# First block: last three output tiles in token halves, norm and new x by halves beneath them, gate-up started by halves, squares added by VectorE

## What is computed

```
mixed = concat(rms_norm(out_a, group_norm_a), rms_norm(out_b, group_norm_b)) @ w_out
x = x + rms_norm(mixed, norm_mix_post)
h = rms_norm(x, norm_ffn_pre)
f = (silu(h @ w_gate) * (h @ w_up)) @ w_down        # 1024 -> 2816 -> 1024
x = x + rms_norm(f, norm_ffn_post)
```

## Time and profile before

| what | value |
|---|---|
| median of 3 runs | 1234.2 us |
| the profiled execution | 1236.36 us |
| its span, first to last instruction | 1234.6 us |
| TensorE matmul busy | 1140.7 us (92%) |
| VectorE busy | 669.2 us (54%) |
| ScalarE busy | 499.5 us (40%) |
| GpSimd busy | 155.5 us (13%) |
| mean granted TensorE clock | 0.973 of full |

### The profile page before, as it was taken

The page is one execution under the profiler, slowest core; times in us unless marked ns, Lnnn a source line. Parts: engine busy times, 40 slices in busy tenths (PEclk is TensorE's granted clock), DMA queues, the critical chain, the costliest instruction groups (busy, mean ns, idle before and its releaser), DMA issues.

```text
span 1234.6 us, 14658 instructions
## 1 busy us (share of the span) xinstructions
PE 1140.7 (92%) x5104; PEld 918.3 (74%) x5104; DVE 669.2 (54%) x1054; ACT 499.5 (40%) x823; POOL 155.5 (13%) x162
## 2 busy tenths in 40 slices
PE   6897968949999999999978998699999999999996
PEld 5675857737888888888856887577888888888884
DVE  6776885677444444433348787736444444443332
ACT  5785776334333232322234366734332323232221
POOL 1475763021000000000003002200000000000001
PEclk9999989969999999999989999989999999999998
DMA  7311100412322222322221221003222222222311
GB/s 255 115 52 44 52 27 1 162 43 76 111 85 102 88 99 102 102 102 102 102 94 36 93 94 69 1 2 136 85 102 102 97 90 101 86 102 103 102 51 68
DMA packets 31465, 106.04 MB, mean 86 GB/s; under 512 B 4032, under 2 KB 4672, under 8 KB 31296
## 3 DMA queue, kind: packets, MB, share of 16 engines
q1 hardware_dynamic: 31088, 104.99, 24.6%
q10 hardware_dynamic: 336, 0.52, 0.2%
HBM read 100.78 MB, written 2.10 MB: 83 GB/s over the span
## 4 chain that ended last, share of the span: by engine, by line
PE 77%; DVE 11%; ACT 6%; issue 4%; DMA 0%; ACTq 0%; DVEq 0%; POOL 0%; SPq 0%
PE bank L456 23%; PE bank L457 23%; PE bank L458 23%; DVE hl L1469 2%; PE bank L897 1%; PE bank L887 1%; DVE ta L1461 1%; ACT wh L370 1%; DVE xres L1463 1%; DVE wl L378 1%; DVE q L1063 1%; DVE pr L952 1%; ACT pr L1398 1%; ACT pr L1100 1%; ACT pth L1086 1%
## 5 line engine op out<-in xcount | busy, mean ns | idle before, releaser
L456 PE MATMUL bank<-hh,wh 128*128 128x512 f32 x936 | 373.4, 399 | 27.5 <-DVE hl L1469 25.7
L378 DVE TENSOR_TENSOR wl<-raw,wh 128x1024 fp32r<-128x1024 f32 x181 | 223.3, 1234 | 322.9 <-ACT wh L370 322.6
L370 ACT ACTIVATE wh<-raw 128x1024 fp32r<-128x1024 f32 x181 | 191.4, 1058 | 448.2 <-PE bank L458 304.6
L457 PE MATMUL bank<-hl,wh 128*128 128x512 f32 x936 | 368.3, 393 | 0.0
L458 PE MATMUL bank<-hh,wl 128*128 128x512 f32 x936 | 367.7, 393 | 0.0
L456 PEld LDWEIGHTS bank<-hh,wh 128*128 128x128 f32 x936 | 177.9, 190 | 71.5 <-issue 24.1
L458 PEld LDWEIGHTS bank<-hh,wl 128*128 128x128 f32 x936 | 178.0, 190 | 38.1
L457 PEld LDWEIGHTS bank<-hl,wh 128*128 128x128 f32 x936 | 178.2, 190 | 37.9 <-issue 1.7
L458 PE MATMUL bank<-gh,wl 128*128 128x512 f32 x352 | 139.0, 395 | 0.0
L456 PE MATMUL bank<-gh,wh 128*128 128x512 f32 x352 | 139.0, 395 | 0.0
L457 PE MATMUL bank<-gl,wh 128*128 128x512 f32 x352 | 139.0, 395 | 0.0
(11 more groups left out here) (209 smaller groups left out, 1392.9 us busy)
## 6 DMA issues: line engine op xcount, KB each, us to landing
raw<-weights SPq DMA_DIRECT2D x181, 512.0 KB, 3.2
xres<-x_t SPq DMA_DIRECT2D x8, 512.0 KB, 6.8
sw<-ta SPq DMA_DIRECT2D x36, 64.0 KB, 2.0
out_t<-final SPq DMA_DIRECT2D x8, 256.0 KB, 2.2
rope<-angles SPq DMA_DIRECT2D x1, 1024.0 KB, 10.8
sw<-ta ACTq DMA_DIRECT2D x4, 64.0 KB, 2.9
wp<-pool_weights ACTq DMA_DIRECT2D x1, 256.0 KB, 3.4
mats_raw<-matrices SPq DMA_DIRECT2D x1, 128.0 KB, 8.9
```

The costliest lines, as they stand in the source:

```text
L370: act.activation(wh[:, j, :, :], raw[:, j, :, :], ACT.Copy).then_inc(high_split, 1)
L378: v.tensor_tensor(wl[:, j, :, :], raw[:, j, :, :], wh[:, j, :, :].bitcast(F32), ALU.subtract)\
L456: pe.matmul(bank[:, :], wh[:, slot, b, :], ah[:, k, :], start=first and n == 0, stop=False)
L457: pe.matmul(bank[:, :], wh[:, slot, b, :], al[:, k, :], start=False, stop=False)
```

## The change

- Tiles 5, 6 and 7 of the output projection are computed in two halves of 256 tokens. The order of the units is tiles 0 to 4 whole, then 5, 6, 7 for the first half of the tokens, then 5, 6, 7 for the second (called 5a, 6a, 7a, 5b, 6b, 7b here).
- VectorE makes the low half of the next chunk behind the tile's own reads, not ahead of them; chunks g0+1, g0+2 and g0+3 are parted later, among the new steps. All other steps of tiles 5 to 7 are on half tiles.
- The sum of squares of the first token half runs on TensorE inside unit 5b, before its blocks 6 and 7; ScalarE makes the first half of `rstd`; VectorE and ScalarE make the new x, `hh` and `hl` of that half while TensorE runs 6b and 7b.
- Gate-up's first group starts on the first token half (`pe_gu1_first`): blocks 0 to 2 with tiles 0 and 1, then tile 2, blocks 3 to 5 with tiles 0 to 2, the sum of squares of the second half, blocks 6 and 7, then tile 3; then the same four tiles for the second half. They lie in banks 3, 0, 1, 2; later groups in banks 4 to 7.
- The squares of the new x go to a buffer of 8 tiles, `sqs`. VectorE adds them in a tree of 7 adds (`vec_sum_squares`). GpSimd's 8 steps go away. Their sum over the partitions runs behind the first tile of group 1, no longer inside the first group.
- gu2 has the bank order and loop of gu1, and parts two chunks ahead of its norm factor, not one.

```diff
-            for d in range(KT):
-                vec_split(v, c0 + d + RING)
...
+            for u in range(5):
+                vec_mix(v, u)
+                if u >= 1:
+                    add_square(v, n_mp, u - 1, acc)
+                vec_mix_add(v, u)
+                vec_split(v, c0 + u + RING)
+            for u in (5, 6, 7):
+                vec_mix(v, u)
...
+            vec_mix(v, 8)
+            vec_mix_add(v, 8)
+            v.wait_ge(n_mh[0].ready, 1)
+            vec_scale(v, 0, 0)
+            vec_split(v, g0 + 1)
+            vec_update(v, 0, 0)
+            vec_scale(v, 1, 0)
+            vec_mix(v, 9)
+            vec_half_square(v, 5, 1)
+            vec_update(v, 1, 0)
+            vec_mix_add(v, 9)
+            for k in range(2, 5):
+                vec_scale(v, k, 0)
+                vec_half_low(v, k - 2, 0)
+                vec_update(v, k, 0)
+                if k == 2:
+                    vec_split(v, g0 + 2)
+            vec_mix(v, 10)
+            vec_half_square(v, 6, 1)
+            vec_mix_add(v, 10)
+            for k in range(5, KT):
+                vec_scale(v, k, 0)
+                vec_half_low(v, k - 2, 0)
+                vec_update(v, k, 0)
+                if k == 5:
+                    vec_split(v, g0 + 3)
+            vec_half_low(v, 6, 0)
+            v.wait_ge(n_mh[1].ready, 1)
+            for k in range(KT):
+                vec_scale(v, k, 1)
+                if k == 0:
+                    vec_half_low(v, 7, 0)
+                if k >= 2:
+                    vec_half_low(v, k - 2, 1)
+                vec_update(v, k, 1)
...
+                for k in range(8):
+                    if UNITS[u] == (5, 1) and k == 6:
+                        half_sum(pe, 0, banks[6])
+                    ins = out_piece(pe, u, k)
...
+            pe_halves(pe, c0, t0, h_ffn1, 0, [(k, j) for k in range(3) for j in range(2)] + [(k, 2) for k in range(3)]
+                      + [(k, j) for k in range(3, 6) for j in range(3)])
+            half_sum(pe, 1, banks[7])
+            pe_halves(pe, c0, t0, h_ffn1, 0, [(k, j) for k in (6, 7) for j in range(3)] + [(k, 3) for k in range(KT)])
+            pe_halves(pe, c0, t0, h_ffn1, 1, [(k, j) for k in range(SPLIT) for j in range(4)]
+                      + [(k, j) for j in range(4) for k in range(SPLIT, KT)])
...
+            act_half_h(act, 5, 0)
+            act_split(act, g0 + 3)
+            act_half_h(act, 6, 0)
+            act_half_rstd(act, 1, banks[7])
+            act_half_h(act, 7, 0)
...
-            for k in range(KT):
-                add_square(g, n_fp, k, acc)
...
+            vec_split(v, CHUNK0["gu1"] + RING)
+            vec_sum_squares(v)
+            vec_split(v, CHUNK0["gu1"] + RING + 1)
```

More of the change, by code:

```diff
@@ new lines, in pe_halves @@
+        def pe_halves(pe, c0, t0, h, half, order):
+            n = HALVES[half]
+            seen_k = -1
+            for k, j in order:
+                slot, bank = (c0 + j) % RING, banks[(t0 + j) % 4]
+                first, last = (half, k) == (0, 0), (half, k) == (1, KT - 1)
+                if first:
+                    slot_wait(pe, c0 + j)
+                if k > seen_k:
+                    pe.wait_ge(h.low, KT * half + k + 1)
+                    seen_k = k
+                pe.matmul(bank[:, n], wh[:, slot, k, :], hh[:, k, n], start=first, stop=False, skip_group_check=True)
+                pe.matmul(bank[:, n], wh[:, slot, k, :], hl[:, k, n], start=False, stop=False, skip_group_check=True)
+                ins = pe.matmul(bank[:, n], wl[:, slot, k, :], hh[:, k, n], start=False, stop=last, skip_group_check=True)
+                if last:
+                    ins.then_inc(used, 1)
@@ L1256, in build @@
         mixed_parts = sem("mixed1_parts")
-        def vec_take1(v):
-            c0 = CHUNK0["out1"]
-            for d in range(KT):
-                vec_split(v, c0 + d + RING)
[L1263 to L1274, removed]
+        first_half = sem("out1_first_halves")
@@ new lines, in vec_scale, with vec_update, vec_half_low @@
+        def vec_scale(v, k, half):
+            n = HALVES[half]
+            v.scalar_tensor_tensor(ta[:, k % 2, n], mixed1[:, k, n], col("mix_post", k), rstd[:, n], ALU.mult, ALU.mult)\
+                .then_inc(x_scaled, 1)
+        def vec_update(v, k, half):
+            n = HALVES[half]
+            v.wait_ge(x_scaled, KT * half + k + 1)
+            v.wait_ge(x_loaded[k // 2], 32)
+            v.tensor_tensor(xres[:, k, n], xres[:, k, n], ta[:, k % 2, n], ALU.add).then_inc(x_new1, 1)
+        def vec_half_low(v, k, half):
+            n = HALVES[half]
+            v.wait_ge(h_ffn1.high, KT * half + k + 1)
+            v.scalar_tensor_tensor(hl[:, k, n], xres[:, k, n], col("ffn_pre", k), hh[:, k, n].bitcast(F32),
+                                   ALU.mult, ALU.subtract).then_inc(h_ffn1.low, 1)
@@ L1486, in build, with pe_gate_up @@
         gu1, gu2 = GateUp("gu1"), GateUp("gu2")
-        def pe_gate_up(pe, gu, h, norm):
-            def group(i):
+        def pe_gate_up(pe, gu, norm, n_added=None):
+            for j in range(4):
+                pe.wait_ge(low_split, gu.c0 + 4 + j + 1)
+                if j == 3:
+                    pe.wait_ge(norm.ready, 1)
+                products(pe, banks[4 + j], (gu.c0 + j) % RING, range(KT), hh, hl, 0, True, True).then_inc(used, 1)
+                if j == 0 and n_added is not None:
+                    sum_squares(pe, norm, n_added, acc, banks[7])
+            with pe.Fori(2, FT // 2) as i:
@@ L1506, in vec_gate_up @@
             v.wait_ge(norm.ready, 1)
[L1507 to L1517 removed]
+            for r in range(2):
+                vec_gate(v, gu, r, banks[(gu.t0 + 2 * r) % 4], banks[(gu.t0 + 2 * r + 1) % 4])
+                vec_product(v, gu, r)
+                vec_split(v, gu.c0 + RING + r + 2)
+                vec_hidden_low(v, gu, r)
@@ L1522, in vec_gate_up, with act_silu, act_hidden_high @@
                     vec_split(v, gu.c0 + RING + 2 * r + 2, i)
-        def act_gate_up(act, gu):
-            with act.Fori(0, FT // 2) as i:
+        def act_silu(act, gu, r, i=0):
+            act.wait_ge(bank_read, gu.t0 + 4 * i + 2 * r + 1)
+            act.activation(tb[:, r, :], ta[:, r, :], ACT.Silu).then_inc(gu.silu, 1)
+        def act_hidden_high(act, gu, r, i=0):
+            f = 2 * i + r
+            act.wait_ge(gu.product, f + 1)
+            act.activation(gh[:, f, :], tb[:, r, :], ACT.Copy).then_inc(gu.hidden.high, 1)
@@ L1741, in _ @@
             pe_out2(pe)
[L1742 removed]
+            pe_gu2_first(pe)
+            pe_gate_up(pe, gu2, n_f2)
             pe_down(pe, "down2", gu2)
```

211 lines of the change are left out of this document (160 added, 51 removed).

## The result

The changed kernel takes **1220.6 us** in the median of four executions (1218.8 to 1223.8), the kernel before 1233.9 in the same series. The ratio is 0.9893, with a 95% interval of 0.9868 to 0.9919, so 1.1% faster, clear of no change. The forecast was 1220.0, in a range from 1215.5 to 1227. The profiled execution of the changed kernel took 1218.82 us with a span of 1216.6.

The account below looks back on a forecast made before the run. TensorE was taken to wait on VectorE and ScalarE between output projection and gate-up; 16.1 us gained at full clock, less 2.0 for the clock and 0 to 0.2 for gu2, gave 1234.2 - 14.2 = 1220.0 us, range 1215.5 to 1227.

Parts of the forecast that it names:

- the 2.0 us put on for the clock: Clock falls after TensorE's idling between 247 and 257.7 us; slower half matmuls and half sum cost 2.0 us, between 0 and 5.
- low part 5 ready: VectorE's low part of block 5, first token half of the new x, ready at 258.8 us after two waits for ScalarE.
- group 1 starts: TensorE finishes gate-up's first group and starts group 1 at 278.5 us.
- part 1: Prices of half steps: VectorE 0.33 and 0.39 us from start to start, half matmuls on TensorE 0.12 us.
- rival 3: Half-width matmuls are paced by weight loads that do not overlap: 18 us more, 1238 us, chance 0.04.
- The two waits for ScalarE: In the new x's first half, VectorE waits at chunks g0+2 and g0+3: about 0.6 and 1.9 us.
- The wait of tile 2 in group 1: In gate-up's group 1, chunk g0+6 comes late and tile 2 waits 0.5 us, between 0 and 1.5.
- rival 4: Gate-up cannot use the earlier start because VectorE is behind; TensorE waits for chunks, 10 us lost again: 1230 us, chance 0.04.
- the 0 to 0.2 for gu2: Deduction from the gain for gu2, where TensorE never waited for its changed bank order and earlier chunks: 0 to 0.2 us.
- rival 1: The clock stays up because idle stretches are shorter than reckoned: 16.1 us gained, 1218 us, chance 0.25.
- GpSimd's part: VectorE's steps making the new x run at lone prices without GpSimd; at contended prices eight blocks end about 8 us later.
- the ring of 5.28 us: In the output projection, ScalarE's square and high half and VectorE's chunk, reads and add take turns, 5.28 us a tile.

Follow-up runs that it names:

- experiment 9: The changed kernel with chunk g0+3 parted behind the first half's block 6, not behind block 5: 1216.9 us, ratio 0.9846 to the kernel before.
- experiment 1: The changed kernel measured again, unedited: 1220.8 us, ratio 0.9889 to the kernel before.
- experiment 3: The kernel before, whole tiles, with the chunk's low half behind the reads and VectorE adding squares in a tree: 1219.9 us, ratio 0.9877.
- experiment 4: The kernel before, in its old order with whole tiles, with VectorE's tree of adds in place of GpSimd's: 1228.7 us, ratio 0.9946.
- experiment 6: The changed kernel with 14 GpSimd adds of 128x256 in place of VectorE's tree: 1220.9 us, ratio 0.9885 to the kernel before.

## Why the prediction was right

**The chain, step by step.** Counted from the group-norm factor (216.92 in the prediction, 216.20 in the profiled execution), in us, and with the predicted steps at the full clock, before the 2.0 us put on for the clock, the steps came out so:

| step | predicted | measured |
|---|---|---|
| VectorE through with its five rounds | 17.1 | 17.1 (233.31) |
| first half sum | 22.6 | 22.4 (238.59) |
| rstd used for the first half | 25.5 | 25.4 (241.57) |
| low part 5 ready | 41.9 | 41.8 (257.99) |
| second half's rstd used | 45.0 | 45.1 (261.25) |
| group 1 starts | 61.6 | 61.6 (277.77) |

The steps of part 1 carry this: VectorE's half steps start 0.33 and 0.39 us apart, with 0.41 and 0.48 to their end, where 0.33 and 0.39, 0.42 and 0.48 were taken from rows of other instructions; half matmuls with a weight load each start 0.12 apart over whole tiles:

```profile
265.89 0.28 PE L985 MATMUL bank<-hh,wh 128*128 128x256 f32 x1
266.01 0.28 PE L986 MATMUL bank<-hl,wh 128*128 128x256 f32 x1
266.13 0.28 PE L987 MATMUL bank<-hh,wl 128*128 128x256 f32 x1
266.25 0.28 PE L985 MATMUL bank<-hh,wh 128*128 128x256 f32 x1
```

That settles rival 3, and with it the 0.21 us by the Trainium skill's figure for a weight load ("TensorE: Matmul & The Clock Gate", "LDWEIGHTS (loading the stationary operand)"), if loads and matmuls added up. They overlap.

**The two waits for ScalarE** were put at 0.6 and 1.9 us and are 0.37 and 1.83. That the second was on the path is what experiment 9 shows; the 3 us for the chunk and its wait came back when it was moved.

**The wait of tile 2 in group 1**, put at 0.5, is 0.26 (from 0.23 to 0.49 between two starts):

```profile
289.36 0.39 PE L468 MATMUL bank<-hh,wl 128*128 128x512 f32 x1
289.85 0.50 PE L466 MATMUL bank<-hh,wh 128*128 128x512 f32 x1
```

With 0.11 in the interval behind it that is all that TensorE waits from group 1 to the down projection, apart from the sum put in, and rival 4 falls. Behind the stretch, where gu2 lies, the profiled executions have 721.0 us before and 719.9 and 722.2 in the changed kernel, so the 0 to 0.2 for gu2 cannot be told from their spread. (One slip of the working: 24 matmuls at the pace of the earlier trace rows, 4.08 us for 18, are 5.44 us a tile, not 5.46. It stands on both sides of the sum.)

**The clock.** Put at 2.0 us, between 0 and 5. In one profiled execution it stayed up (rival 1, stretch 280.5, the 16.1 us of the sum at full clock), in the other it fell, not once but twice, and cost 1.5 (282.0). The reason given, that the clock falls around the waits for low parts and that the work behind them then goes at half pace, holds there; that only work on TensorE's own time costs anything was not in it. So forecast and rival 1 both occur, in different executions of one kernel. The nine times (1218.8 to 1225.4, median 1220.8) do not show the two apart, because most of the difference between its two profiled executions arises outside the stretch (experiment 1). The median of the first series is 0.6 us from the forecast, and that is in part luck: the gain in the medians is 13.3 us in the first series and 15.3 in the second, against 14.2 forecast. The profiled execution was put at a span of 1220.4 and has 1216.6, of which the clock is 1.9; 0.7 lies ahead of the stretch and 1.2 behind it.

**What was mis-sized.** GpSimd's part was given "about 8 us" by way of the row. That was a length of VectorE's list, not a time of the kernel. Measured, the list gets 6.7 us shorter for whole tiles (experiment 3), and the stretch 2.3, or 4.8 in the old order (experiment 4); with halves it is 1.9 and nothing in the median (experiment 6). The sum did not rest on the 8, since it was laid out at lone prices.

**What the prediction did not say.** It took the parts of the change as one, so its being right on the sum says nothing on what pays. Its own first reading, the ring of 5.28 us, when undone alone gives 12.9 of the 16.1 us. Laid out alone in the same way, the order would have shown that the halves, with 1.7 us of dearer matmuls and a VectorE list longer by its short steps, add little once the ring is gone: 1.0 us over order and tree (281.5 to 280.5), and with the clock at 1.00 in both the whole tiles are 1.4 us ahead (279.1 against 280.5, one profiled execution each).

## What to carry to other kernels

Where two engines hand work to each other in turn, look first at what stands in each one's list between two hand-overs: moving one chunk's step behind the reads that others wait for gave here what a rebuild in halves gave. A step that waits for another engine belongs where its own engine would wait anyway. And a shorter list on one engine is worth only what the engine behind it can use: set its time per block against that engine's before counting it. (The same holds for the clock: its first fall in experiment 1 cost nothing, the second 1.5 us.)

## What the hardware showed that was not expected

- Short matmuls into an unused bank, 10 ahead of the norm sum and 24 behind it, left the granted clock at 1.00 through a stretch in which nothing else could run, and the stretch was 2.5 us shorter. With 12 behind the sum and 2.41 us of waiting after them it read 0.98 there and 0.74 in the 6 us behind, when TensorE was busy again.
- GpSimd adds of 128x256 take 0.73 to 1.14 us, and of the VectorE half steps beside them one to an add took 0.94 to 0.96 in place of 0.42 to 0.48, beside ten of the 14 adds; beside the other four none did. What decides which step it is, no run here shows.
